# Two transformer output projections on one NeuronCore: weights loaded during attention, high parts moved ahead of squares, norm sums one unit sooner

## What is computed

```python
for i in range(DEPTH):
    h = _rmsnorm(x, norm_mix[i])
    if i % N_MIXERS == 0:
        mix = _swa_sink_mixer(h, swa_w_in[j], swa_sinks[j], swa_w_out[j], cos, sin)
    else:
        mix = _fox_mixer(h, fox_w_in[j], fox_f_bias[j], fox_w_out[j])
    x = x + mix.astype(x.dtype)
    h = _rmsnorm(x, norm_ffn[i])
    x = x + _swiglu(h, ffn_w_gate_up[i], ffn_w_down[i]).astype(x.dtype)
return _rmsnorm(x, norm_final)
```

## Time and profile before

| | us |
|---|---|
| Median of 3 runs | 2486.77 |
| Lowest and highest | 2485.86, 2491.13 |
| The profiled execution | 2491.87 |
| Its span | 2490.1 |
| TensorE busy in it | 2339.4 |
| VectorE, ScalarE, GpSimd busy | 1398.7, 987.2, 589.5 |

### The profile page before, as it was taken

One profiled execution on the slowest core, in us unless ns is written; L12 is line 12 of the kernel. 1 busy time (PEld: TensorE's weight loads), 2 busy tenths in 40 slices (PEclk: granted clock), 3 DMA queues, 4 the chain that ended last, 5 costly groups with the idle time before them and its releaser, 6 DMA issues.

```text
span 2490.1 us, 33386 instructions
## 1 busy us (share of the span) xinstructions
PE 2339.4 (94%) x11220; PEld 1930.0 (78%) x11220; DVE 1398.7 (56%) x2204; ACT 987.2 (40%) x1884; POOL 589.5 (24%) x419
## 2 busy tenths in 40 slices
PE   4998979899999999999999989989889999999998
PEld 3776767688888878887888778877678888878887
DVE  7797954864544443433633489994584444453432
ACT  3116953443333331232212289983343333331223
POOL 3222431233322200020000056652222233200011
PEclk8999999999999999999999999999989999999999
DMA  5258543232222162222444587746313222334311
GB/s 186 89 160 207 107 135 103 68 102 76 76 89 88 59 242 92 88 97 74 144 136 152 174 189 173 173 94 194 110 51 100 77 76 80 97 127 165 114 51 76
DMA packets 306742, 291.82 MB, mean 117 GB/s; under 512 B 64992, under 2 KB 270176, under 8 KB 301680
## 3 DMA queue, kind: packets, MB, share of 16 engines
q1 hardware_dynamic: 286464, 233.99, 33.0%
q10 hardware_dynamic: 20208, 56.92, 6.2%
HBM read 209.02 MB, written 81.85 MB: 117 GB/s over the span
## 4 chain that ended last, share of the span: by engine, by line
PE 77%; DVE 14%; ACT 4%; issue 2%; DMA 2%; POOL 1%; ACTq 1%; SPq 0%; DVEq 0%
PE psum L1986 11%; PE psum L1988 11%; PE psum L1990 11%; PE psum L1738 10%; PE psum L1739 10%; PE psum L1740 10%; PE psum L1872 2%; DVE work_b L1629 2%; PE psum L1964 2%; PE psum L1890 2%; PE psum L1965 2%; PE psum L1966 2%; PE psum L1891 1%; PE psum L1839 1%; PE psum L1840 1%
## 5 line engine op out<-in xcount | busy, mean ns | idle before, releaser
L1986 PE MATMUL psum<-b_hi,a_hi 128*128 128x512 f32 x1232 | 484.8, 393 | 20.1 <-DVE b_lo L1457 20.1
L1988 PE MATMUL psum<-b_lo,a_hi 128*128 128x512 f32 x1232 | 482.8, 392 | 0.0
L1990 PE MATMUL psum<-b_hi,a_lo 128*128 128x512 f32 x1232 | 482.6, 392 | 0.0
L1986 PEld LDWEIGHTS psum<-b_hi,a_hi 128*128 128x128 f32 x1232 | 233.4, 189 | 71.8 <-issue 23.0
L1738 PE MATMUL psum<-set_hi,dw_hi 128*128 128x512 f32 x704 | 274.7, 390 | 3.1 <-DVE set_lo L1491 3.1
L1740 PE MATMUL psum<-set_hi,dw_lo 128*128 128x512 f32 x704 | 273.9, 389 | 0.0
L1739 PE MATMUL psum<-set_lo,dw_hi 128*128 128x512 f32 x704 | 273.9, 389 | 0.0
L1990 PEld LDWEIGHTS psum<-b_hi,a_lo 128*128 128x128 f32 x1232 | 233.4, 189 | 49.4
L1988 PEld LDWEIGHTS psum<-b_lo,a_hi 128*128 128x128 f32 x1232 | 233.6, 190 | 48.6 <-issue 0.4
L716 POOL TENSOR_TENSOR score<-score,inv_l 128x128 f32<-128x128 f32 (+7 forms) x128 | 155.2, 1223 | 379.8 <-DVE inv_l L1323 379.6
L750 POOL TENSOR_TENSOR a_sum<-a_raw 128x512 f32<-128x512 f32 x88 | 115.8, 1316 | 508.6 <-DVE a_lo L1452 440.2
(11 more groups left out here) (207 smaller groups left out, 4437.3 us busy)
## 6 DMA issues: line engine op xcount, KB each, us to landing
a_raw<-in_ffn_w_gate_up SPq DMA_DIRECT2D x88, 512.0 KB, 5.1
hid_scr<-hid_out SPq DMA_DIRECT2D x44, 512.0 KB, 5.7
set_full<-hid_scr SPq DMA_DIRECT2D x22, 1024.0 KB, 6.5
x_t<-x_scr SPq DMA_DIRECT2D x16, 1024.0 KB, 7.2
dw_raw<-in_ffn_w_down SPq DMA_DIRECT2D x32, 512.0 KB, 4.1
x_scr<-x_t ACTq DMA_DIRECT2D x24, 512.0 KB, 2.6
w_raw<-in_fox_w_in SPq DMA_DIRECT2D x22, 512.0 KB, 4.0
w_raw<-in_swa_w_out SPq DMA_DIRECT2D x16, 512.0 KB, 4.1
```

The costliest lines, as they stand in the source:

```text
L1986: T.matmul(out_ps, a_hi[i][:, j, :], b_hi[i][:, j, :], start=not more and j == 0, stop=False, skip_group_check=True)
L1988: T.matmul(out_ps, a_hi[i][:, j, :], b_lo[i][:, j, :], start=False, stop=False, skip_group_check=True)
L1990: last = T.matmul(out_ps, a_lo[i][:, j, :], b_hi[i][:, j, :], start=False, stop=j == KH - 1, skip_group_check=True)
```

## The change

Four moves, in both projections. The two strips for units 2 and 3 are loaded ahead of the reload of x_t, behind the last attention unit's loads. On ScalarE the high part of unit j + 2 stands ahead of the square of unit j. TensorE takes the first half's sums after unit 8. VectorE makes the diagonal in its unit 9. (The first hunk only keeps the attention's name.)

```diff
         class Attention:
             def __init__(self, name):
-                self.fox = name == "fox"
+                self.name, self.fox = name, name == "fox"
...
             def load_out(c0, view, layer):
-                for j in range(2, 4):
-                    load_out_w(c0, view, j)
-
                 sp.wait_ge(mm_done, 2 * (c0 + 1))
                 load_a(layer, 0, 0)
                 load_a(layer, 1, 1)
...
                 k = 2 if a.fox else 0
+                for j in range(2, 4):
+                    load_out_w(C_O1 if a.fox else C_O0, w_out_view[a.name], j)
                 sp.wait_ge(a.pv_done, a.groups * a.units - 1)
                 sp.dma_start(x_t[:, 0:2, :], x_scr[:, 0:2, :]).then_inc(x_back[k], 16)
...
                     h, m = j // KD, j % KD
+                    if j < 2 * KD - 2:
+                        high(c0 + j + 2, j % 2)
                     act.wait_ge(evac_done, 2 * (c0 + j) + 2)
...
                         act.dma_start(x_scr[:, m, :], x_t[:, m, :]).then_inc(x_stored, 16)
-                    if j < 2 * KD - 2:
-                        high(c0 + j + 2, j % 2)
                     if 0 <= j - 2 < NP:
                         weight_high(r0, 0, j - 2)
...
-                    if j == KD + 2:
+                    if j == KD + 1:
                         norm_diag(k, 0)
...
-                    if j == KD + 1:
+                    if j == KD:
                         norm_sums(k, 0)
                     if j == KD + 2:
                         norm_bc(k, 0)
```

## The result

| | before | changed kernel |
|---|---|---|
| median of 4 runs on one chip, us | 2487.55 (2485.86 to 2491.13) | 2463.71 (2460.73 to 2466.71) |
| profiled execution, us (its span) | 2491.9 (2490.1) | 2460.73 (2458.9) |
| busy us: TensorE, VectorE, ScalarE, GpSimd | see above | 2329.7, 1409.0, 987.2, 600.2 |

The ratio is 0.9902, with a 95% interval of 0.9883 to 0.9921: some 24 us faster, where 26.5 were forecast; 2463.71 lies in the range on record. The profiled execution before is slower than all four of its runs, the one after is the fastest of its four. They are 31.1 us apart: the two projections are 26.2 us shorter, and the rest lies where nothing was changed: 2.6 us before the first projection, 1.2 between the two and 1.1 behind the second. Over the ten profiles of this study these three stretches vary by 4.4, 2.8 and 1.2 us.

A forecast was written before the change was run, and what follows sets the result against it. TensorE was taken as the bound almost everywhere, so only its pauses could yield time. Terms 3.9 + 4.9 + 16.7 + 1.0 = 26.5 us off the 2486.8 median gave 2460.3 us, range 2452 to 2469.

The forecast's parts named there:

- first projection: unit 4 earlier, less the low clock behind the wait: Unit 4 starts at 373.3 instead of 378.86, 5.6 us, less 1.7 of low clock: 3.9 us, bounds 2 and 8.
- second projection: unit 4 earlier: Unit 4 starts at 1707.2 instead of 1712.05: 4.9 us gained, bounds 3.5 and 6.5.
- the two norms: TensorE's wait for the diagonal and the low clock behind it go in both projections: 8.8 and 7.9 us.
- unit 15: The small wait before unit 15 and the delays of chained low parts go: 1.0 us.
- from last byte to use I take 2: First projection, unit 4's strip: 2 us from landing at 368.0 to its high part at 370.0.
- Ready at T + 5.2: The norm's diagonal is ready 5.2 us after T, the end of unit 9.
- 0.25 us to spare: Slack of the diagonal, ready at T + 5.2, before unit 10 ends at T + 5.44.
- rival (b): Diagonal late: 1 us of wait and 3 of low clock per projection; 18.5 us gained, 2468; chance 0.12.
- (a): The wait only moves to unit 4, which starts no earlier; 17.7 us gained, 2469; chance 0.12.
- (c): No low clock after short waits and strips in time; 32.5 us gained, 2454; chance 0.15.
- (d): Gain given back at the FFN's first products, which wait longer; no change, 2487; chance 0.02.
- (e): Longer unbroken TensorE work brings the lower clock; one projection's matmuls would cost 77 us, 2537; chance 0.01.

The follow-up runs named there:

- e5: The changed kernel once more, unaltered, as partner of later runs: 2461.28 us, ratio 0.9895.
- e1: The kernel before with only the strips of units 2 and 3 loaded ahead of x_t: 2484.0 us, ratio 0.9981.
- e2: The kernel before with only ScalarE's high parts put ahead of the squares: 2483.47 us, ratio 0.9976.
- e8: The changed kernel with the diagonal back at its old place in VectorE's unit 10: 2475.55 us, ratio 0.9953.
- e3: The kernel before with only the norm's steps moved, sums after unit 8 and diagonal in unit 9: 2474.17 us, ratio 0.9942.
- e4: The changed kernel with TensorE's sums left at their old place behind unit 9: 2463.85 us, ratio 0.9898.
- e7: The changed kernel with unit 4's strip loaded between the two pairs of a_raw loads: 2455.14 us, ratio 0.9866.
- e6: The changed kernel with unit 4's strip loaded ahead of all four a_raw strips: 2461.94 us, ratio 0.9894.

## Why the prediction was right

The number held because each wait was read from its own releaser, and the terms came out one by one, here against the first profile:

| term, us | forecast | measured |
|---|---|---|
| first projection: unit 4 earlier, less the low clock behind the wait | 5.6 - 1.7 = 3.9 | 4.54 - 1.59 = 2.95 |
| second projection: unit 4 earlier | 4.9 | 4.95 |
| the two norms | 8.8 and 7.9 | 8.87 and 8.02 |
| unit 15 | 1.0 | 1.45 |
| sum | 26.5 | 26.24 |

That the sums agree to 0.3 us is partly luck: by e5's profile of the same kernel the two projections are 28.2 us shorter, and inside the first term errors of 1 to 2 us cancel, as follows.

*Loads earlier, high parts ahead.* Right in mechanism: waits of 1.11 and 1.79 us before unit 2 were forecast as 1.1 and 1.9. e1 shows that without the high parts the wait is 2.39, and e2 that without the loads it is 7.1: for unit 2 both moves are needed. The new wait before unit 4, forecast as 3.5, was 4.24. Two errors stand behind that. The step "from last byte to use I take 2" put the high part 12.64 us behind unit 1's last matmul (370.0 - 357.36). It came at 14.59 in the first profile and at 12.66 in e5's, so the step is good only to 2 us. The transfer rates of the changed kernel (below) show a hole of two slices near 361 us, deeper than that of the earlier trace rows. In the same stretch of e5, counted from unit 1's last matmul, the lowest slice of the strips has 119 GB/s, not 26. That the hole is what made the strip late is not shown. The rates of the changed kernel in 40 slices of 350 to 374 us:

```profile
GB/s 246 382 423 410 410 410 382 423 410 355 410 410 343 339 352 304 288 303 91 26 192 269 332 225 190 292 292 269 318 324 325 282 188 68 0 0 0 9 161 247
```

And the low part, which I took at 2.2 us beside GpSimd, took 1.23, as VectorE began it at 370.41 and GpSimd its next add at 370.54. So the high part came 2.0 us late and the low part was 1.0 us short, and the two errors partly cancel. In the second projection the low part did meet that work, and took 2.16 at the change and 2.21 in e5:

```profile
1687.87 3.52 POOL L769 TENSOR_TENSOR ssq_ffn<-ssq_ffn,sq_ffn 128x512 f32<-128x512 f32 x2
...
1688.08 2.16 DVE L1225 TENSOR_TENSOR w_lo<-w_raw,w_hi 128x1024 fp32r<-128x1024 f32 x1 [1.77 <-ACT w_hi L823]
```

That is about what the earlier trace rows gave. Beside the rule of the Trainium skill (SBUF — State Buffer, Who interferes with whom), I had put it at up to 3.1, a whole add of 1.8 lost; that is not seen. It does not speak against the rule: the low part began 0.21 us into an add that takes 1.29 alone, and lost 0.93 us, a little less than was left of that add; nat_t in e8, which ended with the add that it met, agrees too. The 1.8 was half of 3.60 in the earlier trace rows, where the first of the two adds had itself begun beside a low part and took 2.23.

*The norms.* The largest term, and the closest. "Ready at T + 5.2" came at 413.27 - 408.19 = 5.08, but the product, which the prediction had at T + 5.44, could start at 413.36 - 408.19 = 5.17, so that "0.25 us to spare" was 0.09. With such a slack it is luck, and not the working, that decided between the forecast and rival (b). Rival (b), the late diagonal, did not come true, but e3 shows how near it is: with the high part behind the square the diagonal misses by 0.54 us. I had charged such a miss with 3 us of low clock; e3 had none. What does the work is the step on VectorE (e8), not the sums on TensorE (e4), though the diff moves both and the prediction's term is named after the sums. Moving the sums is what makes the slack so small: where they stay (e4), 1.20 us are to spare and the time is the same. Alone, e1, e2 and e3 shorten the projections by 6.4 + 5.7 + 15.5 = 27.6 us; the change does so by 26.2, and by 28.2 in e5. So the three parts very nearly add up.

*Rivals.* (a), the wait only moves to unit 4, is half true: it did move there in the first projection, at 4.24 us, but unit 4 still came 4.54 and 4.95 us sooner. (c), no low clock after short waits and the strips in time, failed on the strips; on the clock it was right for some short waits and wrong for others (last section). (d) is refuted by b_lo's unchanged 5.4 us. (e) did not occur: the granted clock's mean over the run is 0.975 to 0.982. The Trainium skill (TensorE: Matmul & The Clock Gate, HAM oscillation), by which only long idle gaps bring the lower clock, agrees with the 1.11 us waits and with the row at 372.34, at 0.63 us a matmul after a wait of 4.24. The lower clock after 1.79 us in two profiles (last section) does not fit it, and there the measurement decides.

*The median.* It is 3.4 us above the forecast of 2460.3. The wait before unit 4 explains part of such a spread: 4.24, 4.1, 2.36 and 3.57 us in the profiles of the change, e4, e5 and e8, where its source is the same. I did not settle what sets the landing from run to run.

## What to carry to other kernels

Where an engine works in order, ask of the instruction that TensorE is waiting for what stands in front of it and for what that waits: here seven short VectorE operations behind an evacuation cost 15 us (e8), and ScalarE copies of 1 us, each behind a square, another 5 (e2). When one wait is removed, work out when the next strip lands, and place its load between the loads that feed the next chain, not before or behind them all (e7 against e6 and the change). Move only what something waits for: work that stands between two units also hides what must be ready behind the second, and moving the sums forward cut a slack of 1.20 us to 0.09 for nothing (e4). Price a pause of some microseconds on TensorE at its length and, as a range, the low-clock stretch behind it, and let no step rest on a slack of 0.1 us without a measured margin.

## What I had not expected of the hardware

*The clock after short waits.* Unit 2's wait of 1.11 us was followed by the lower clock in none of six profiles (the change, e4 to e8). The second projection's wait of 1.79 us was, in two of the same six (the change and e8: units 2 to 3 took 7.2 us, otherwise 5.6). Of the longer waits in the first projection, those of 2.36 to 4.24 us before unit 4 or 5 were followed by it every time: in the change, e1, e5 and e6 by seven or eight matmuls 0.43 us apart, some 1.6 us lost, in e4 and e8 by eleven and twelve, 2.5 and 2.7 us lost; yet e1's wait of 2.39 us before unit 2 was not, and e6's of 1.81 in the second projection was. At the start of the changed kernel's first FFN, waits of 1.92 and 1.91 us (for b_lo) were followed by it too. So between 1.8 and 2.4 us the length of the wait alone does not tell, and I had made a sure cost of it from the single case of the earlier trace rows. What else decides was not tried. In the second projection it hardly mattered: where the clock stayed up (e4, e5), unit 4 waited 1.21 and 1.25 us for its strip and began at 14.6, against 14.8 with the low clock.

*VectorE beside GpSimd.* The small low part of an a_raw strip takes 0.68 us in the first projection of before, and mostly 1.6 to 1.8 with the high part ahead; GpSimd's add beside it goes from 1.29 to 1.81. e1 and e3, which leave the high part behind the square, keep the 0.68, and e2, which moves nothing else, has the 1.8. Timeline of the changed kernel:

```profile
370.54 3.94 POOL L769 TENSOR_TENSOR ssq_ffn<-ssq_ffn,sq_ffn 128x512 f32<-128x512 f32 x2
...
371.67 1.67 DVE L1451 TENSOR_TENSOR a_lo<-a_raw,a_hi 128x512 fp32r<-128x512 f32 x1
```

The two run at the same moment now. Over the run VectorE is busy 10.3 us more (1398.7 to 1409.0) and GpSimd 10.7 us more (589.5 to 600.2), with not one instruction added. In e1 and e3 VectorE stays at 1398.0 and 1397.4, in e2 it is 1410.2. The low parts of the a_raw strips lie off the path. That of unit 4's strip does not: in the second projection of e4 and e5 it took 2.21 us beside GpSimd, where 1.23 is its time alone, and TensorE waited 1.21 and 1.25 us for it. It is the kind of price that a count of instructions does not show.
